# Stationary operands woven in pairs of blocks, and split weights placed at 128 modulo 256 bytes

## The chip, the cores and the metric

The kernel runs on one core of one Trainium2 chip. The metric is the device time of one execution in microseconds (us), as the median of several runs. Before the change it is 778.98 us (three runs, 777.98 to 779.29).

## The reference: what is computed

One encoder layer is applied to two sequences of 256 tokens with 1024 channels, all in fp32. The kernel treats them as one block of 512 tokens.

```
x = layer_norm(x)
z = x @ w_in + b_in                      # 1024 -> 3584, split into q, k, v, u_sg, v_sg, glu_a, glu_g
a = neighbourhood_attention(q, k, v) @ w_a_o
bb = (gelu(u_sg) * (w_s @ layer_norm(gelu(v_sg)) + b_s)) @ w_b_o
c = silu(layer_norm(conv31(glu_a * sigmoid(glu_g)))) @ w_c_o
g = sigmoid(x @ w_gate + b_gate)         # three gates of 1024
m = (g0 * a + g1 * bb + g2 * c) @ w_o + b_o
x = layer_norm(ALPHA * x + m)
f = top-2 of 16 experts (one group of 4): sum of gate_e * ((silu(x @ w_e1[e]) * (x @ w_e3[e])) @ w_e2[e])
y = layer_norm(ALPHA * x + f)
```

## The kernel before, in words

**One product is three.** The large products keep fp32 accuracy by splitting. A value x becomes `hi`, x rounded to the type fp32r, and `lo` = x - hi, also fp32r. A product is then hi·hi + hi·lo + lo·hi. The helper `three` issues these three matmuls in that order into one PSUM bank, 512 columns wide. Each matmul has its own load of the stationary operand, a block of 128 x 128 elements of 4 bytes, so 512 bytes in each partition. The moving operand has 128 x 512 elements, 2048 bytes in each partition.

**Weights come in units.** A unit is 1024 elements in each partition (512 KB in all). SyncE loads it into a raw buffer. ScalarE rounds it into a slot of `w_hi` (`cast_hi`, copy on L719), VectorE subtracts it into a slot of `w_lo` (`cast_lo`, L1055), and TensorE uses it. There are three slots of `w_hi` and `w_lo` for the mixer and a fourth (`w_hi_more`, `w_lo_more`) for the experts. Semaphores order the four: a raw buffer is loaded again after `lo_cast`, a slot is rounded into again after `unit_used`, and TensorE waits for `lo_cast` of the unit. The raw buffers are 6 in the mixer and a ring of 24 in the experts.

**Two ways of using a unit.** In `features` (units of the glu, q, k, u_sg, the gates and the branch projections) the weight is the stationary operand and the activation (`xT_hi`, `xT_lo`, `branch_hi`, `branch_lo`) is the moving one. A unit then holds eight blocks of 128 x 128. In `tokens` (units of v, v_sg, w_o and all experts) the weight is the moving operand, two chunks of 512 columns, and the activation is stationary: `xT_hi`/`xT_lo` for v and v_sg, `mT_hi`/`mT_lo` for w_o, `xgT_hi`/`xgT_lo` (the gathered tokens of an expert, transposed) for the first two matrices of an expert, `hT_hi`/`hT_lo` for the third.

**Where the operands lie.** Every stationary block is 128 elements next to one another. All the operands of `three` ask for an address that is a multiple of 256 bytes (`LINE = 256`), apart from `mT_lo` and the third branch, and blocks and chunks are multiples of 512 bytes apart.

**The order of work.** TensorE first transposes the input, then runs the units of `w_in` 0 to 27 (glu, v, v_sg, q and k, u_sg) with the attention and the spatial gating woven in between. Then come the gates and branches (`merge`, units 28 to 63), w_o (units 64 to 71), the router, and the 16 experts. An expert is 12 units of 6 matmuls, with two transposes of activations in between: `turn_xg` (L2137, eight of 128 columns) and `turn_h` (L2152, four). Their results are split by ScalarE (`split_xg` L932, `split_hT` L943) and VectorE (L1541, L1551). All orders are written out by hand, and each engine works through its own list in order. The depthwise convolution (31 taps, L1125) is done by VectorE in pieces between its weight subtractions.

The lines that the prediction speaks of: L1842 to L1844 (`three`), L1055 and L719 (the splits of weights), L2097 (`keep_busy`, matmuls whose result is not used, before the experts), L1985 (a plain fp32 product with `ones` for the mean of the convolution's normalisation), L565 (SyncE's loads), L1837 (`turn`, here the transposed softmax), L1888 (`attend`), L745 (ScalarE's sigmoid of the glu).

Of the kernel before, what the change touches and what calls it, by code (L numbers as in the profile page):

```python
# [56 lines left out]
LINE = 256  # L57
UNIT = 1024
# [103 lines left out]
def encoder_layer(nc, A, out_prompt, out_sample):  # L162
# [20 lines left out]
    w_hi = sb(ctx, "w_hi", [SPLIT, UNIT], F32R, LINE)  # L183
    w_lo = sb(ctx, "w_lo", [SPLIT, UNIT], F32R, LINE)
# [51 lines left out]
    mT_hi = sb(late, "mT_hi", [DC, T], F32R, LINE)  # L236
    mT_lo = sb(late, "mT_lo", [DC, T], F32R)
# [64 lines left out]
    list_row = sb(moe, "list_row", [EXPERTS], I32)  # L302
    list_gate = sb(moe, "list_gate", [EXPERTS])
    list_none = sb(moe, "list_none", [2, 4])
    list_base = sb(moe, "list_base", [2, 4])
    w_hi_more = sb(moe, "w_hi_more", [M_SPLIT - SPLIT, UNIT], F32R, LINE)
    w_lo_more = sb(moe, "w_lo_more", [M_SPLIT - SPLIT, UNIT], F32R, LINE)
# [5 lines left out]
    xgT_hi = sb(moe, "xgT_hi", [2, DC, SLOTS], F32R, LINE)  # L313
    xgT_lo = sb(moe, "xgT_lo", [2, DC, SLOTS], F32R, LINE)
    h_silu = sb(moe, "h_silu", [FF])
    h = sb(moe, "h", [FF])
    hT_hi = sb(moe, "hT_hi", [4, SLOTS], F32R, LINE)
    hT_lo = sb(moe, "hT_lo", [4, SLOTS], F32R, LINE)
# [102 lines left out]
    last_hT_hi, last_hT_lo = xgT_hi[:, 0, 0:4, :], xgT_lo[:, 0, 0:4, :]  # L421
# [276 lines left out]
    def _(act):  # L698
# [11 lines left out]
        def cast_hi(j, per=0, i=None):  # L710
# [8 lines left out]
            act.copy(hi_slot(j), raw_slot(j)).then_inc(hi_cast, 1)  # L719
# [117 lines left out]
        def merged_hi_rows(r):  # L837

            for c in (2 * r, 2 * r + 1):
                act.wait_ge(merged_ready, c + 1)  # L840
                act.copy(mT_hi[:, c, :], merged[:, c, :]).then_inc(merged_hi, 1)
# [99 lines left out]
        def split_hT(n, hT_hi=hT_hi[:]):  # L941
            act.wait_ge(*m_filled(M_HT, n))
            act.copy(hT_hi.rearrange("p c n -> p (c n)"), psum[M_HT][:]).then_inc(hT_hi_done, 1)  # L943
# [101 lines left out]
    def _(dve):  # L1045
# [37 lines left out]
        dve.tensor_copy(hi_slot(0), raw_slot(0)).then_inc(first_hi, 1)  # L1083
        dve.wait_ge(first_hi, 1)
        dve.tensor_tensor(lo_slot(0), raw_slot(0), hi_slot(0).bitcast(F32), ALU.subtract).then_inc(lo_cast, 1)
# [212 lines left out]
        def merged_lo_rows(r):  # L1298

            for c in (2 * r, 2 * r + 1):  # L1300
                dve.wait_ge(merged_hi, c + 1)
                dve.tensor_tensor(mT_lo[:, c, :], merged[:, c, :], mT_hi[:, c, :].bitcast(F32),
# [234 lines left out]
        def split_xg(n, q):  # L1537
            for half in range(2):
                dve.wait_ge(xg_hi, n * 2 + (half + 1))
                part_of = (slice(None), q, slice(4 * half, 4 * half + 4))  # L1540
                dve.tensor_tensor(xgT_lo[part_of], psum[M_XT + half][:].rearrange("p (c n) -> p c n", c=4),  # L1541
                                  xgT_hi[part_of].bitcast(F32), ALU.subtract).then_inc(psum_free[M_XT + half], 1)
# [6 lines left out]
        def split_hT(n, hT_hi=hT_hi[:], hT_lo=hT_lo[:]):  # L1549
            dve.wait_ge(hT_hi_done, n + 1)  # L1550
            dve.tensor_tensor(hT_lo.rearrange("p c n -> p (c n)"), psum[M_HT][:],  # L1551
                              hT_hi.rearrange("p c n -> p (c n)").bitcast(F32),
# [274 lines left out]
    def _(pe):  # L1827
# [18 lines left out]
        def features(j, outs, x_hi, x_lo, per=0, i=None):  # L1846

            pe.wait_ge(lo_cast, nth(j + 1, per, i))
            hi, lo = unit_of(hi_slot(j), len(outs) * P), unit_of(lo_slot(j), len(outs) * P)
            chunks = UNIT // (len(outs) * P)  # L1850
            for d, name in enumerate(outs):
                open_bank(name, i)
                cols = slice(d * P, (d + 1) * P)
                for c in range(chunks):
                    o = three(bank(name)[:], hi[:, c, cols], lo[:, c, cols], x_hi[:, c, :], x_lo[:, c, :],
# [3 lines left out]
        def tokens(j, k, last, outs, x_hi, x_lo, choose, per=0, i=None):  # L1859
# [3 lines left out]
            for t, out in enumerate(outs):  # L1863
                for c in range(2):
                    o = three(out, choose(x_hi[:, 2 * k + c, :], t), choose(x_lo[:, 2 * k + c, :], t), hi[:, c, :],
# [26 lines left out]
        def in_row(x, t):  # L1892
            return x[:, tokens_of(t)]

# [419 lines left out]
```

## Time and profile before

| | |
|---|---|
| median of three runs | 778.98 us |
| the profiled execution: its time | 777.9 us |
| its span, first to last instruction | 776.1 us |
| PE busy | 745.4 us (96%), 3516 matmuls |
| PEld (weight loads) busy | 616.5 us (79%) |
| DVE busy | 609.9 us (79%) |
| ACT busy | 432.6 us (56%) |
| mean granted TensorE clock | 0.992 |

PE is TensorE's matmuls and PEld its weight loads, DVE is VectorE, ACT ScalarE, POOL GpSimd and SPq the queue of SyncE. A matmul's recorded duration overlaps the next one, so the pace of the stream is read from the distance between starts, not from the durations. Of the 3516 matmuls 2880 are from `three`.

### The profile page before, as it was taken

What the parts mean: (1) busy time and instruction counts of PE and PEld (TensorE: products, weight loads), DVE (VectorE), ACT (ScalarE), POOL (GpSimd) and SP (SyncE); (2) the same over time, 40 slices, a digit from 0 to 9 for tenths busy, and PEclk for the clock granted to TensorE, in tenths of its full rate; (3) what the DMA queues carried; (4) which work ended last, traced back from release to release, by engine and by line L of the source; (5) the groups of instructions that cost most, each with busy time, mean ns of one, the idle gap of its engine ahead of it and who ended that gap; (6) DMA issues with size and microseconds to landing.
All of it is one profiled execution on the core that took longest, in us unless ns stands there. A gap on an engine that the chain in (4) does not pass through costs nothing.

```text
span 776.1 us, 10638 instructions
## 1 busy us (share of the span) xinstructions
PE 745.4 (96%) x3516; PEld 616.5 (79%) x3516; DVE 609.9 (79%) x827; ACT 432.6 (56%) x585; POOL 72.0 (9%) x96
## 2 busy tenths in 40 slices
PE   4999999999999999999999979999999999999995
PEld 3888877887888888888888857888888888888873
DVE  5799977777678857444348888999999999999977
ACT  5522235657322335422421456888888888888851
POOL 5000000000000000000011121111111111110314
PEclk9999999999999999999999989999999999999998
DMA  9744657232343452332388587999999999999682
GB/s 297 238 98 108 204 147 205 71 93 84 109 134 109 112 167 74 115 103 88 104 303 300 186 302 255 351 392 379 388 386 389 391 400 384 381 394 378 146 171 111
DMA packets 137489, 175.51 MB, mean 226 GB/s; under 512 B 15419, under 2 KB 75559, under 8 KB 137431
## 3 DMA queue, kind: packets, MB, share of 16 engines
q1 hardware_dynamic: 128896, 154.95, 58.8%
q0 software_dynamic: 7616, 19.34, 8.3%
q10 hardware_dynamic: 934, 0.69, 0.3%
q8 instruction: 23, 0.38, 0.2%
q14 instruction: 20, 0.16, 0.1%
HBM read 164.06 MB, written 19.11 MB: 236 GB/s over the span
## 4 chain that ended last, share of the span: by engine, by line
PE 85%; DVE 8%; DMA 2%; ACT 2%; SPq 2%; issue 1%; POOL 0%; DVEq 0%; ACTq 0%; POOLq 0%
PE bank L1842 25%; PE bank L1844 25%; PE bank L1843 25%; DVE w_lo L1055 2%; PE bank L2137 2%; DMA raw<-in_w_in_dram 2%; SPq L606 1%; DVE conv L1125 1%; DVE conv_odd L1125 1%; PE bank L2058 1%; PE bank L1837 1%; PE bank L2152 1%; PE bank L2238 1%; PE bank L1888 1%; PE bank L1904 1%
## 5 line engine op out<-in xcount | busy, mean ns | idle before, releaser
L1055 DVE TENSOR_TENSOR w_lo<-raw,w_hi 128x1024 fp32r<-128x1024 f32 x103 | 125.0, 1220 | 77.2 <-ACT w_hi L719 77.1
L719 ACT CAST w_hi<-raw 128x1024 fp32r<-128x1024 f32 x103 | 107.0, 1048 | 101.5 <-PE bank L1844 97.6
L1842 PE MATMUL bank<-xT_hi,w_hi 128*128 128x512 f32 x352 | 138.5, 393 | 2.7 <-DVE xT_lo L1093 1.5
L1844 PE MATMUL bank<-xT_hi,w_lo 128*128 128x512 f32 x352 | 137.1, 390 | 0.0
L1843 PE MATMUL bank<-xT_lo,w_hi 128*128 128x512 f32 x352 | 137.0, 389 | 0.0
L1842 PE MATMUL bank<-w_hi,xgT_hi 128*128 128x512 f32 x198 | 80.1, 405 | 1.0 <-issue 1.0
L1842 PEld LDWEIGHTS bank<-xT_hi,w_hi 128*128 128x128 f32 x352 | 66.1, 188 | 17.3 <-issue 3.1
L1844 PE MATMUL bank<-w_hi,xgT_lo 128*128 128x512 f32 x198 | 77.5, 391 | 0.0
L1843 PE MATMUL bank<-w_lo,xgT_hi 128*128 128x512 f32 x198 | 77.3, 390 | 0.0
L1844 PEld LDWEIGHTS bank<-xT_hi,w_lo 128*128 128x128 f32 x352 | 66.1, 188 | 14.0
L1843 PEld LDWEIGHTS bank<-xT_lo,w_hi 128*128 128x128 f32 x352 | 66.1, 188 | 13.4
L834 ACT ACTIVATE gate<-bank,vec 128x512 f32<-128x512 f32 x24 | 16.5, 689 | 83.2 <-PE bank L1844 83.2
L1055 DVE TENSOR_TENSOR w_lo<-raw_more,w_hi 128x1024 fp32r<-128x1024 f32 x40 | 48.2, 1221 | 5.7 <-ACT w_hi L719 5.4
L1055 DVE TENSOR_TENSOR w_lo<-raw_late,w_hi 128x1024 fp32r<-128x1024 f32 x40 | 48.2, 1220 | 4.1 <-ACT w_hi L719 3.9
L1125 DVE SCALAR_TENSOR_TENSOR conv<-conv_in,conv_col,conv 128x512 f32<-128x512 f32 x60 | 44.6, 744 | 0.0
L719 ACT CAST w_hi<-raw_more 128x1024 fp32r<-128x1024 f32 x40 | 41.2, 1049 | 4.5 <-PE bank L1844 4.5
L1844 PEld LDWEIGHTS bank<-w_hi,xgT_lo 128*128 128x128 f32 x198 | 37.2, 188 | 7.9
L1842 PEld LDWEIGHTS bank<-w_hi,xgT_hi 128*128 128x128 f32 x198 | 37.3, 188 | 7.8 <-issue 1.2
L719 ACT CAST w_hi<-raw_late 128x1024 fp32r<-128x1024 f32 x40 | 41.2, 1050 | 2.5 <-PE bank L1844 2.5
L1843 PEld LDWEIGHTS bank<-w_lo,xgT_hi 128*128 128x128 f32 x198 | 37.3, 188 | 6.6
L1125 DVE SCALAR_TENSOR_TENSOR conv_odd<-conv_in,conv_col,conv_odd 128x512 f32<-128x512 f32 x56 | 41.6, 744 | 0.0
L1055 DVE TENSOR_TENSOR w_lo<-raw_rows,w_hi 128x1024 fp32r<-128x1024 f32 x32 | 38.3, 1218 | 0.0
(289 smaller groups left out, 1530.9 us busy)
## 6 DMA issues: line engine op xcount, KB each, us to landing
raw_more<-in_w_e_dram SPq DMA_DIRECT2D x48, 512.0 KB, 7.0
raw<-in_w_e_dram SPq DMA_DIRECT2D x48, 512.0 KB, 7.9
raw_late<-in_w_e_dram SPq DMA_DIRECT2D x48, 512.0 KB, 7.1
raw_rows<-in_w_e_dram SPq DMA_DIRECT2D x48, 512.0 KB, 7.9
raw<-in_w_in_dram SPq DMA_DIRECT2D x28, 512.0 KB, 6.5
raw<-in_w_gate_dram SPq DMA_DIRECT2D x24, 512.0 KB, 3.7
y_scratch<-zeros SPq DMA_DIRECT2D x8, 512.0 KB, 5.3
raw<-in_w_o_dram SPq DMA_DIRECT2D x8, 512.0 KB, 3.8
```

The costliest lines, as they stand in the source:

```text
L606: sp.dma_start(v_win[:, seq, j, :], v_grid[:, WINDOW[j]:WINDOW[j] + KCOLS, :]).then_inc(v_windows, 16)
L719: act.copy(hi_slot(j), raw_slot(j)).then_inc(hi_cast, 1)
L834: act.activation(gate[:, n if n < 2 else r % 2, d, :], bank(name)[:], ACT.Sigmoid, bias=column(V_GATE + n * DC + 2 * r + d)).then_inc(free ...
L1055: dve.tensor_tensor(lo_slot(j), raw_slot(j), hi_slot(j).bitcast(F32), ALU.subtract).then_inc(lo_cast, 1)
L1125: o = dve.scalar_tensor_tensor(out=sum_, in0=shifted, scalar=conv_col[:, k, c:c + 1], in1=sum_, op0=ALU.mult, op1=ALU.add)
L1837: o = pe.transpose(bank(name)[:, k * P:(k + 1) * P], tile(k), ident)
L1842: pe.matmul(out, hi_l, hi_r, start=start, stop=False)
L1843: pe.matmul(out, hi_l, lo_r, start=False, stop=False)
L1844: return pe.matmul(out, lo_l, hi_r, start=False, stop=stop)
L1888: o = pe.matmul(bank(("attended", g))[:, j * P:(j + 1) * P], v_win[:, seq, j, hp * P:(hp + 1) * P], probsT[:, j * P:(j + 1) * P], start=Tr ...
L1904: o = pe.transpose(bank(name)[:, tokens_of(t)], x_in[:, t, c * P:(c + 1) * P], ident)
L2137: o = pe.transpose(psum[M_XT + half][:, k * P:(k + 1) * P], xg[:, q, c * P:(c + 1) * P], ident)
```

## The change

Two blocks of a stationary operand are stored element by element: element n of block 2k lies at 2n and element n of block 2k+1 at 2n+1. A load of one block then reads every second element, 128 elements over 1024 bytes. This holds for the weights of `features` (they are woven where they are split) and for `mT_hi`, `xgT_hi`, `xgT_lo`, `hT_hi` and `hT_lo`. The stationary operands `xT_hi`, `xT_lo` (for v and v_sg) and `mT_lo` stay as they were, and so do the weights where they are moving operands. `w_hi`, `w_lo`, `w_hi_more` and `w_lo_more` now ask for a multiple of 128 bytes; with the order in which they are placed they lie at 128 modulo 256. All other operands of `three` stay at multiples of 256.

```diff
+APART = 128
-    w_hi = sb(ctx, "w_hi", [SPLIT, UNIT], F32R, LINE)
-    w_lo = sb(ctx, "w_lo", [SPLIT, UNIT], F32R, LINE)
+    w_hi = sb(ctx, "w_hi", [SPLIT, UNIT], F32R, APART)
+    w_lo = sb(ctx, "w_lo", [SPLIT, UNIT], F32R, APART)
-    mT_hi = sb(late, "mT_hi", [DC, T], F32R, LINE)
-    mT_lo = sb(late, "mT_lo", [DC, T], F32R)
+    mT_hi = sb(late, "mT_hi", [DC // 2, T, 2], F32R, LINE)
+    mT_lo = sb(late, "mT_lo", [DC, T], F32R, LINE)
...
-    xgT_hi = sb(moe, "xgT_hi", [2, DC, SLOTS], F32R, LINE)
+    xgT_hi = sb(moe, "xgT_hi", [2, DC // 2, SLOTS, 2], F32R, LINE)
-    hT_hi = sb(moe, "hT_hi", [4, SLOTS], F32R, LINE)
+    hT_hi = sb(moe, "hT_hi", [2, SLOTS, 2], F32R, LINE)
...
+    def is_stationary(j):
+        return j < U_V or U_QK <= j < U_WO
+    def woven(slot):
+        return slot.rearrange("p (k n b) -> p k b n", b=2, n=P)
+    def split_of(slot, j):
+        return woven(slot) if is_stationary(j) else slot
+    def raw_of(j):
+        return raw_slot(j).rearrange("p (k b n) -> p k b n", b=2, n=P) if is_stationary(j) else raw_slot(j)
+    def chunk(tile, c):
+        return tile[:, c // 2, :, c % 2]
+    def by_chunk(tile):
+        return tile.rearrange("p k n b -> p k b n")
...
-            act.copy(hi_slot(j), raw_slot(j)).then_inc(hi_cast, 1)
+            act.copy(split_of(hi_slot(j), j), raw_of(j)).then_inc(hi_cast, 1)
...
-            dve.tensor_tensor(lo_slot(j), raw_slot(j), hi_slot(j).bitcast(F32),
+            dve.tensor_tensor(split_of(lo_slot(j), j), raw_of(j), split_of(hi_slot(j).bitcast(F32), j),
...
-                act.copy(xgT_hi[:, q, 4 * half:4 * half + 4, :],
-                         psum[M_XT + half][:].rearrange("p (c n) -> p c n", c=4)).then_inc(xg_hi, 1)
+                act.copy(by_chunk(xgT_hi[:, q, 2 * half:2 * half + 2]),
+                         psum[M_XT + half][:].rearrange("p (k b n) -> p k b n", k=2, b=2)).then_inc(xg_hi, 1)
...
-            hi, lo = unit_of(hi_slot(j), len(outs) * P), unit_of(lo_slot(j), len(outs) * P)
+            hi, lo = woven(hi_slot(j)), woven(lo_slot(j))
...
-                    o = three(bank(name)[:], hi[:, c, cols], lo[:, c, cols], x_hi[:, c, :], x_lo[:, c, :],
+                    at = (slice(None), *divmod(len(outs) * c + d, 2))
+                    o = three(bank(name)[:], hi[at], lo[at], x_hi[:, c, :], x_lo[:, c, :],
                               c == 0, c == chunks - 1)
...
-            tokens(j, k, k == 3, [psum[b][:]], xgT_hi[:, q], xgT_lo[:, q], lambda x, t: x, per, i)
+            tokens(j, k, k == 3, [psum[b][:]], chunks_of(xgT_hi[:, q]), chunks_of(xgT_lo[:, q]), whole, per, i)
```

The splits of `mT`, `xgT_lo` and `hT` are changed in the same way. No instruction is added, taken away or moved, and no semaphore changes.

## Rows read from the trace of the kernel before

**Rows 1.** The page, busy time and share of the span by engine.
```profile
PE 745.4 (96%) x3516; PEld 616.5 (79%) x3516; DVE 609.9 (79%) x827; ACT 432.6 (56%) x585; POOL 72.0 (9%) x96
```

**Rows 2.** Waits of PE: engine, line, releaser: us in total, times, longest.
```profile
PE bank L1888 <- DVE branch_lo L1169: 1.8, 1, 1.8
...
PE bank L1837 <- DVE probs L1162: 1.0, 1, 1.0
```

**Rows 3.** Groups of PE by line: busy, mean ns, idle before and its releasers.
```profile
L1842 PE MATMUL bank<-xT_hi,w_hi 128*128 128x512 f32 x352 | 138.5, 393 | 2.7 <-DVE xT_lo L1093 1.5 <-DVE vs L1217 1.0 <-DVE w_lo L1055 0.2
```

**Rows 4.** Timeline of PE (start us, us), 24 matmuls in a row, first and last.
```profile
225.21 0.39 PE L1842 MATMUL bank<-branch_hi,w_hi 128*128 128x512 f32 x1
...
230.43 0.39 PE L1844 MATMUL bank<-branch_hi,w_lo 128*128 128x512 f32 x1
```

**Rows 5.** Timeline of PE, one unit of `features` behind a transpose.
```profile
140.83 0.40 PE L1843 MATMUL bank<-xT_lo,w_hi 128*128 128x512 f32 x1
...
141.53 0.39 PE L1843 MATMUL bank<-xT_lo,w_hi 128*128 128x512 f32 x1
141.75 0.39 PE L1844 MATMUL bank<-xT_hi,w_lo 128*128 128x512 f32 x1
...
142.91 0.39 PE L1843 MATMUL bank<-xT_lo,w_hi 128*128 128x512 f32 x1
...
144.95 0.39 PE L1843 MATMUL bank<-xT_lo,w_hi 128*128 128x512 f32 x1
```

**Rows 6.** Timeline of PE, a plain fp32 product's two records.
```profile
274.17 0.59 PE L1985 MATMUL bank<-conv_ln,const 128*128 128x512 f32 x1
...
274.60 0.59 PE L1985 MATMUL bank<-conv_ln,const 128*128 128x512 f32 x1
```

**Rows 7.** Timeline of PE, two looks at L2097, five starts apart.
```profile
462.78 1.05 PE L2097 MATMUL bank<-w_hi 128*128 128x512 f32 x2
...
464.91 1.05 PE L2097 MATMUL bank<-w_hi 128*128 128x512 f32 x2
```

**Rows 8.** Windows, L2097 alone: PE busy (x), PEld busy (x), PEclk, DMA share, GB/s.
```profile
463.30:465.90 2.60, 2.60 (x8) 2.02 (x7) 0.50 0.54 148
```

**Rows 9.** Timeline of PE, eight transposes of 128 columns.
```profile
466.41 1.03 PE L2137 MATMUL bank<-const,xg 128*128 128x128 f32 x8
```

**Rows 10.** Windows by stage, L1842 alone, columns as in rows 8.
```profile
20.00:63.00 43.00, 24.48 (x63) 11.82 (x63) 1.00 0.58 160
63.00:131.00 68.00, 37.39 (x96) 17.83 (x95) 1.00 0.62 173
131.00:172.00 41.00, 16.09 (x40) 7.52 (x40) 1.00 0.31 91
...
190.00:431.00 241.00, 136.39 (x348) 65.34 (x348) 1.00 0.46 144
431.00:468.00 37.00, 4.88 (x12) 2.25 (x12) 0.91 0.68 244
468.00:752.00 284.00, 152.19 (x384) 72.18 (x384) 1.00 0.98 351
```

**Rows 11.** Chain that ended last, 18 to 110 us and 110 to 200 us.
```profile
63.12 0.70 ACT tmp L745
...
105.34 13.78 DMA raw<-in_w_in_dram
...
172.28 1.34 ACT probs L771 x7
```

**Rows 12.** Windows, all engines (PE, PEld, DVE, ACT, POOL busy), a stretch of experts.
```profile
550.00:600.00 50.00, 50.00 (x236) 41.60 (x235) 46.81 (x49) 43.12 (x52) 5.04 (x5) 1.00 1.03 389
```

**Rows 13.** Waits of SyncE's queue.
```profile
SPq L565 <- DVE w_lo L1055: 378.9, 178, 9.3
```

**Rows 14.** Groups by line, columns as in rows 3.
```profile
L2137 PE MATMUL bank<-const,xg 128*128 128x128 f32 x128 | 16.5, 272 | 0.0
...
L1055 DVE TENSOR_TENSOR w_lo<-raw,w_hi 128x1024 fp32r<-128x1024 f32 x103 | 125.0, 1220 | 77.2 <-ACT w_hi L719 77.1
```

More of the change, by code:

```diff
@@ L418, in encoder_layer @@
     out_stored = sem("out_stored")
[L421 removed]
+    last_hT_hi, last_hT_lo = xgT_hi[:, 0, 0:2], xgT_lo[:, 0, 0:2]
     turned = [next_turned[:, 0], onehot[:, 1]]
@@ L1539, in split_xg @@
                 dve.wait_ge(xg_hi, n * 2 + (half + 1))
-                part_of = (slice(None), q, slice(4 * half, 4 * half + 4))
-                dve.tensor_tensor(xgT_lo[part_of], psum[M_XT + half][:].rearrange("p (c n) -> p c n", c=4),
-                                  xgT_hi[part_of].bitcast(F32), ALU.subtract).then_inc(psum_free[M_XT + half], 1)
+                part_of = (slice(None), q, slice(2 * half, 2 * half + 2))
+                dve.tensor_tensor(by_chunk(xgT_lo[part_of]),
+                                  psum[M_XT + half][:].rearrange("p (k b n) -> p k b n", k=2, b=2),
+                                  by_chunk(xgT_hi[part_of].bitcast(F32)),
+                                  ALU.subtract).then_inc(psum_free[M_XT + half], 1)
         def gate_h(unit, n):
@@ L1864, in tokens @@
                 for c in range(2):
-                    o = three(out, choose(x_hi[:, 2 * k + c, :], t), choose(x_lo[:, 2 * k + c, :], t), hi[:, c, :],
+                    o = three(out, choose(x_hi(2 * k + c), t), choose(x_lo(2 * k + c), t), hi[:, c, :],
                               lo[:, c, :], k == 0 and c == 0, last and c == 1)
@@ L1893, in in_row, with whole, chunks_of, rows_of @@
             return x[:, tokens_of(t)]
+        def whole(x, t):
+            return x
+        def chunks_of(tile):
+            return lambda c: chunk(tile, c)
+        def rows_of(tile):
+            return lambda c: tile[:, c, :]
         pe.wait_ge(const_loaded, 16)
@@ L1925, in first_units @@
                 open_bank(name)
-            hi, lo = unit_of(hi_slot(u), P), unit_of(lo_slot(u), P)
+            hi, lo = woven(hi_slot(u)), woven(lo_slot(u))
             for c in chunks:
                 pe.wait_ge(*drained(("x0T", c)))
-                o = three(bank(name)[:], hi[:, c, :], lo[:, c, :], xT_hi[:, c, :], xT_lo[:, c, :], c == 0,
+                o = three(bank(name)[:], hi[:, c // 2, c % 2], lo[:, c // 2, c % 2], xT_hi[:, c, :], xT_lo[:, c, :], c == 0,
                           c == DC - 1)
@@ L1948, in _ @@
                         open_bank(("v", t))
-                tokens(u, u - U_V, u == U_V + 3, [bank(("v", t))[:] for t in range(TT)], xT_hi, xT_lo, in_row)
+                tokens(u, u - U_V, u == U_V + 3, [bank(("v", t))[:] for t in range(TT)],
+                       rows_of(xT_hi), rows_of(xT_lo), in_row)
             elif u < U_QK:
@@ L1953, in _ @@
                         open_bank(("vsg", t))
-                tokens(u, u - U_VSG, u == U_VSG + 3, [bank(("vsg", t))[:] for t in range(TT)], xT_hi, xT_lo, in_row)
+                tokens(u, u - U_VSG, u == U_VSG + 3, [bank(("vsg", t))[:] for t in range(TT)],
+                       rows_of(xT_hi), rows_of(xT_lo), in_row)
             elif u < U_USG:
@@ L2016, in _ @@
                 pe.wait_ge(merged_lo, 2 * k + 2)
-                tokens(U_WO + 4 * n + k, k, k == 3, [bank(("mixed", n, t))[:] for t in range(TT)], mT_hi, mT_lo,
-                       in_row)
+                tokens(U_WO + 4 * n + k, k, k == 3, [bank(("mixed", n, t))[:] for t in range(TT)],
+                       chunks_of(mT_hi), rows_of(mT_lo), in_row)
         def mix_out(t):
@@ L2027, in mix_out @@
                 for c in range(2):
-                    o = three(bank(name)[:], in_row(mT_hi[:, 2 * k + c, :], t), in_row(mT_lo[:, 2 * k + c, :], t),
+                    o = three(bank(name)[:], in_row(chunk(mT_hi, 2 * k + c), t), in_row(mT_lo[:, 2 * k + c, :], t),
                               hi[:, c, :], lo[:, c, :], False, k == 3 and c == 1)
@@ L2160, in output @@
                 pe.wait_ge(*m_empty(M_Y + k // 2, n))
-            tokens(j, k % 2, k % 2 == 1, [psum[M_Y + k // 2][:]], hT_hi, hT_lo, lambda x, t: x, per, i)
+            tokens(j, k % 2, k % 2 == 1, [psum[M_Y + k // 2][:]], chunks_of(hT_hi), chunks_of(hT_lo), whole, per, i)
         pe.wait_ge(routed, 1)
```

24 lines of the change are left out of this document (12 added, 12 removed).

## The prediction

> **What bounds the kernel now.** I read the busy times first: TensorE is busy for 745.4 of 776.1 us [rows 1]. Then its waits: two in the middle are 1.8 and 1.0 us [rows 2], and its largest group waited for a split of weights for 0.2 us in all [rows 3]. So nothing feeds TensorE too late, and the pace of its own stream sets the time. The pace stands in the timeline, as the distance between starts. Over 24 matmuls of `three` it is (230.43 - 225.21) / 23 = 226.9 ns [rows 4]. 512 columns at the full clock of 2.4 GHz are 213.3 ns, so each pair of load and matmul takes about 13.5 ns more than its columns. 2880 pairs times that are 39 us. This is all that the change can reach, since no instruction goes.
>
> **What the excess is.** Three readings bear on it.
> First, it is absent at half clock. L2097 has the same pairs with its weights contiguous, the granted clock there is 0.50 [rows 8], and five starts take 464.91 - 462.78 = 2.13 us, 426 ns each [rows 7], which is 512 columns at 1.2 GHz and nothing more. A fixed price for changing the weights would show there too.
> Second, it isn't constant. Behind a transpose nine starts take 142.91 - 140.83 = 2.08 us, 231 ns each, with one of 220 (141.53 to 141.75), and the next nine 144.95 - 142.91 = 2.04 us, 227 ns each [rows 5]. Same shapes, same operands: what differs is when the load runs relative to the matmul.
> Third, where no new weights are needed between two passes of 512 columns, it is nearly gone. A plain fp32 product's two records are 430 ns apart [rows 6], which I take as two passes on the same weights: 215 ns each.
> All three fit two reads of the on-chip memory that get into each other's way while a weight load runs beside a matmul. Eight transposes of 128 columns take 1.03 us [rows 9]; without the last one's duration of 0.272 [rows 14] the seven steps are 108 ns each, where 128 columns would take 53. So a load takes about 107 ns and walks its 512 bytes at 4.8 bytes per ns, while the moving operand is walked at 4 bytes x 2.4 GHz = 9.6. Two walks at unequal speed, both from multiples of 256 bytes, must pass through each other.
>
> The Trainium skill says otherwise: by "TensorE: Matmul & The Clock Gate", section "Step-by-step: what each phase is for", the streaming operand and the weight load have independent read ports, and the load of the next weights takes no read bandwidth from the running matmul. By that the excess would be something else and the change would leave it at 226.9 ns and the time at 779. The rows on phase and clock [rows 5, 7] speak against it; it stands below as the case of no change.
>
> **The change part by part.**
> 1. The weave. A load of 128 elements now covers 1024 bytes in the same 107 ns: 9.6 bytes per ns, the moving operand's own speed. With the split weights at 128 modulo 256 and the other operand at 0, the two reads stay 128 bytes apart modulo 256 all the way, if they start together. Woven are all stationary blocks but those of v and v_sg (192 pairs) and `mT_lo` (64). If memory is split by that bit of the address, they never meet, and the pair falls to the 215 ns of [rows 6]: 226.7 - 215 = 11.7 ns gained (226.7 for the steady steps, between 226.9 and 226.7 of [rows 4] and [rows 5]). Bounds: 13.4 ns gained (bare columns); below, a loss of 11.7, if the price goes by the memory that a load touches, which doubles. I take 11.7, as the row of passes without a load is the nearest to a load that meets nothing.
> 2. Where the gain arrives. L1842 is a third of the pairs, so its loads by stage [rows 10] times three: 20 to 63 us: 189; 131 to 172: 120; 190 to 431: 1044, less the 64 of `mT_lo` 980; 431 to 468: 36; 468 to 752: 1152. Sum 2477, times 11.7 ns = 29.0 us.
> 3. Where it doesn't. From 63.12 the chain runs through ScalarE, then VectorE's convolution and SyncE's and the DMA's work until 119.1 (105.34 + 13.78) [rows 11], and ends in the softmax's wait of 1.0 us [rows 2]. None of that gets faster, so the 285 pairs in 63 to 131 (95 of them woven) only make that wait longer. The same holds from 172.28 [rows 11], where ScalarE and VectorE carry the chain to the wait of 1.8 us [rows 2]: 48 pairs, 0.6 us. I count both at nothing; cover that is gone can't hurt, as TensorE is the one that comes early.
> 4. The splits. `cast_hi`, `cast_lo` and the splits of `mT`, `xgT` and `hT` write every second element. A weight subtraction takes 1220 ns [rows 14] for 1024 contiguous elements; the trace has no written stride of this kind. Bounds: nothing, or twice the time. In the mixer a unit of 24 matmuls lasts 24 x 215 = 5.2 us, and TensorE waited 0.2 us for splits [rows 3], so 1.2 us more is mostly hidden, at most some us in the convolution's stage. Among the experts the weights are not woven; only six splits of 512 elements are. I take nothing.
> 5. What is late next. Among the experts VectorE is busy for 46.81 of 50 us [rows 12]. The stage of 284 us gets shorter by 1152 x 11.7 ns = 13.5 us, 4.7%, so VectorE's share rises from 94% to about 98%: it still fits, barely. SyncE waits 378.9 us in all for a free raw buffer [rows 13], so the loads run ahead by a full ring, and 389 GB/s needn't rise at once for weights to be there in time. I add nothing, and keep 2 us of the range for it.
>
> **The sum.** 777.9 (the profiled execution) - 29.0 = 748.9 us. The median of the runs lies 1.1 us above that execution, so 750.0 us.
>
> **The rivals.**
> - *Doubling.* The price goes by the lines of memory that a load touches, each of which holds up the matmul. A contiguous load touches 512 bytes for 11.7 ns, a woven one 1024 for 23.4. It decides if the two walks collide although they are 128 bytes apart. Pair: 238.4 ns. The 2477 pairs cost 29.0 us more, the 95 and 48 of part 3 1.7: 777.9 + 30.7 + 1.1 = 809.7 us, slower. For it: the excess is near to one cycle of 2.4 GHz for each 16 bytes of a load (32 x 0.417 = 13.3). Against it: such a price would be the same at every phase, and [rows 5] has 220 and more than 231 side by side.
> - *Half.* The walks start out of step, and part of each load still collides: half the gain, 14.5 us, 764.5 us.
> - *Nothing.* The excess belongs to the change of weights in the array at full clock, whatever the addresses: 779.0 us. For it: it is so steady at 226.7 for hundreds of pairs. Against it: the half clock.
> - *Slower splits.* Writes of every second element hold VectorE up between the end of v_sg and 131 us, where the chain goes through its splits: six woven units x 1.2 us = up to 7.2 us, and without a gain in the pairs that gives 786 us. It needs both, a split twice as long and no gain.
>
> Of the doubling the Trainium skill says, in "SBUF — State Buffer", section "Specifications (TRN2)", that lines are of 16 bytes and at least two hits in each give full bandwidth. Every second fp32 element is two hits in a line: by that rule a woven load is still at full speed, but at its edge. The trace of before has no strided load to show it.
>
> **How the numbers follow.** The forecast has a chance of 0.52, half 0.10, nothing 0.15, doubling 0.17, slower splits 0.06. So faster 0.62, same 0.15, slower 0.23; 0.2% (1.6 us) is about what a measurement of this kernel can tell from no change. The forecast's own range is 743 (13.4 ns on 2477 pairs is 33.2 us, with the unsteady steps gone another 2) to 755 (the experts' VectorE at 2 us, a rest of 1.5 ns in each pair). The range of 8 in 10 reaches from 743 over half and nothing to 784; the doubling and the worst of the splits lie outside.
>
> **What would show it.** Right: starts of L1842 to L1844 about 215 ns apart at 225 us and among the experts, but still near 227 in v and v_sg (63 to 106 us) or less if the shift by 128 alone helps; longer waits of PE at L1837 and L1888; VectorE's share near 98% among the experts. Doubling would show as 238 ns at full clock; nothing as 226.7 with the same waits; slower splits as longer L1055 and L719 and a wait of L1842 for `w_lo`. The forecast is wrong if the distance of starts does not fall where blocks are woven.

## The result, and the profile after

| | before | after |
|---|---|---|
| median | 778.95 us | 792.0 us |
| lowest to highest of four runs | 777.98 to 779.29 | 791.63 to 792.44 |
| span of the profiled execution | 776.1 us | 789.8 us |
| ratio, 95% interval | | 1.017, 1.0152 to 1.0187 |

The change makes the kernel 13.1 us slower, where 29 us of gain were forecast (750.0 us, with a range of 743 to 784).

The profile's page has the busy times of the changed kernel, which answer to [rows 1]. As many matmuls and loads as before; TensorE is busy for 13.6 us more, VectorE and ScalarE for a little more.

```profile
PE 759.0 (96%) x3516; PEld 638.5 (81%) x3516; DVE 611.5 (77%) x827; ACT 438.0 (55%) x585; POOL 72.0 (9%) x96
```

The waits of TensorE, which answer to [rows 2], are no longer than they were; of its others two at the start grew, from 9.5 to 9.7 us for `x_in` and from 1.5 to 1.8 us for `xT_lo`. So the time did not go into a new wait.

```profile
PE bank L1916 <- DVE branch_lo L1195: 1.8, 1, 1.8
...
PE bank L1865 <- DVE probs L1188: 0.7, 1, 0.7
```

The pace is where it went. The timeline of TensorE (start, duration, both in us) shows, by their first and last matmuls, a stretch of v, whose stationary operand is not woven; the stretch of `features` of [rows 4]; and a stretch among the experts. Before and behind the latter stand two landmarks, the experts' first transposes and the first product behind the experts. In these lines the moving operand is named first and the stationary one second.

```profile
80.09 0.40 PE L1870 MATMUL bank<-w_hi,xT_hi 128*128 128x512 f32 x1
...
83.83 0.40 PE L1871 MATMUL bank<-w_lo,xT_hi 128*128 128x512 f32 x1
...
225.39 0.39 PE L1870 MATMUL bank<-xT_hi,w_hi 128*128 128x512 f32 x1
...
230.70 0.39 PE L1872 MATMUL bank<-branch_hi,w_lo 128*128 128x512 f32 x1
...
475.03 1.38 PE L2176 MATMUL bank<-const,xg 128*128 128x128 f32 x8
...
501.77 0.39 PE L1872 MATMUL bank<-w_hi_more,hT_lo 128*128 128x512 f32 x1
...
504.55 0.39 PE L1872 MATMUL bank<-w_hi,xgT_lo 128*128 128x512 f32 x1
...
766.48 1.02 PE L2277 MATMUL bank<-x,const 128*128 128x512 f32 x2
```

In v, 16 steps take 3.74 us, 233.8 ns each. In `features`, 23 steps take 230.70 - 225.39 = 5.31 us, 230.9 ns each, where [rows 4] has 226.9. Among the experts, 12 steps take 2.78 us, 231.7 ns each. The durations (0.39) hardly tell of it; the starts do.

The two landmarks place the loss. The transposes stood at 466.41 in [rows 9], so 8.6 us are lost ahead of the experts. The first product behind them (here L2277, before L2238) is at 752.67 in the timeline of before, so 13.8 us are lost by then, 5.2 of them among the experts: 1152 pairs at 4.5 ns each.

About one of the 8.6 us comes of the clock and not of where the operands lie. The windows of TensorE show the same stretch before and after (length, busy time and count, granted clock, DMA share, GB/s):

```profile
18.36:21.77 3.41, 3.19 (x13) 1.00 1.07 299
...
18.36:21.77 3.41, 3.41 (x9) 0.50 1.01 290
```

In the profiled execution of the changed kernel nine steps run there at some 427 ns, the pace of a granted clock of 0.50. The transposes of `w_s`, which follow, come at 29.73 us before and at 30.94 after, but at 29.87 in the first experiment below, which weaves too and has a granted clock of 1.00 in this stretch. The second experiment has such a stretch, the others don't. No run shows whether the change brings it about.

The other engines. The splits keep pace: the weight subtraction takes 1222 ns, where [rows 14] has 1220, and from 250 to 400 us, where nearly all of it is woven, 1224 against 1222. ScalarE's rounding of weights (L744) takes 1112 ns in the same stretch, where the unwoven one took 1043. VectorE waits for it a little longer (82.7 us in all, 77.1 in [rows 14]), but TensorE waits for neither. Among the experts VectorE is busy for 45.81 of 50 us (46.81 in [rows 12]), since its work is spread over more time, and SyncE's wait for raw buffers is 390.8 us (378.9 in [rows 13]).

```profile
L1080 DVE TENSOR_TENSOR w_lo<-raw,w_hi 128x1024 fp32r<-128x1024 f32 x103 | 125.2, 1222 | 83.5 <-ACT w_hi L744 82.7
```

```profile
L744 ACT CAST w_hi<-raw 128x1024 fp32r<-128x1024 f32 x27 | 30.0, 1112 | 25.7 <-PE bank L1872 25.7
```

```profile
550.00:600.00 50.00, 50.00 (x234) 42.58 (x233) 45.81 (x48) 42.60 (x51) 6.05 (x6) 1.00 1.02 372
```

```profile
SPq L590 <- DVE w_lo L1080: 390.8, 178, 9.4
```

### The profile page after: what moved, and what is told of

Same layout as the page of the kernel before. It is cut to its first block, busy times and chain, and to the rows that moved or that the text cites. A ratio compares the mean times of both kernels' runs of the same rounds, so it can differ in the third digit from the quotient of the medians.

```text
span 789.8 us, 10638 instructions
## 1 busy us (share of the span) xinstructions
PE 759.0 (96%) x3516; PEld 638.5 (81%) x3516; DVE 611.5 (77%) x827; ACT 438.0 (55%) x585; POOL 72.0 (9%) x96
## 4 chain that ended last, share of the span: by engine, by line
PE 92%; DVE 4%; ACT 2%; issue 1%; DMA 1%; POOL 0%; ACTq 0%; DVEq 0%; POOLq 0%
PE bank L1870 27%; PE bank L1871 27%; PE bank L1872 27%; PE bank L2176 2%; PE bank L2097 1%; PE bank L1865 1%; PE bank L2191 1%; PE bank L2277 1%; PE bank L1916 1%; PE bank L1941 1%; DVE w_lo L1080 1%; DMA x_in<-in_x_prompt_dram 1%; PE bank L2136 1%; PE bank L1906 1%; ACT w_hi L744 1%
## 5 line engine op out<-in xcount | busy, mean ns | idle before, releaser
L1080 DVE TENSOR_TENSOR w_lo<-raw,w_hi 128x1024 fp32r<-128x1024 f32 x103 | 125.2, 1222 | 83.5 <-ACT w_hi L744 82.7
L744 ACT CAST w_hi<-raw 128x1024 fp32r<-128x1024 f32 x103 | 111.2, 1089 | 102.9 <-PE bank L1872 100.6
L1870 PE MATMUL bank<-xT_hi,w_hi 128*128 128x512 f32 x352 | 140.4, 399 | 2.8 <-DVE xT_lo L1119 1.8
L1871 PE MATMUL bank<-xT_lo,w_hi 128*128 128x512 f32 x352 | 139.3, 396 | 0.0
L1872 PE MATMUL bank<-xT_hi,w_lo 128*128 128x512 f32 x352 | 139.1, 395 | 0.0
L1870 PEld LDWEIGHTS bank<-xT_hi,w_hi 128*128 128x128 f32 x352 | 69.3, 197 | 15.7 <-issue 3.4
L1872 PEld LDWEIGHTS bank<-xT_hi,w_lo 128*128 128x128 f32 x352 | 69.4, 197 | 12.7
L1871 PEld LDWEIGHTS bank<-xT_lo,w_hi 128*128 128x128 f32 x352 | 69.3, 197 | 12.1
L1080 DVE TENSOR_TENSOR w_lo<-raw_late,w_hi 128x1024 fp32r<-128x1024 f32 x40 | 48.2, 1222 | 5.2 <-ACT w_hi L744 4.4
L1872 PEld LDWEIGHTS bank<-w_hi,xgT_lo 128*128 128x128 f32 x198 | 38.9, 196 | 7.1
L744 ACT CAST w_hi<-raw_more 128x1024 fp32r<-128x1024 f32 x40 | 41.0, 1045 | 4.7 <-PE bank L1872 4.7
L744 ACT CAST w_hi<-raw_late 128x1024 fp32r<-128x1024 f32 x40 | 41.1, 1047 | 2.7 <-PE bank L1872 2.7
```

The costliest lines, as they stand in the source:

```text
L744: act.copy(split_of(hi_slot(j), j), raw_of(j)).then_inc(hi_cast, 1)
L1080: dve.tensor_tensor(split_of(lo_slot(j), j), raw_of(j), split_of(hi_slot(j).bitcast(F32), j), ALU.subtract).then_inc(lo_cast, 1)
L1870: pe.matmul(out, hi_l, hi_r, start=start, stop=False)
L1871: pe.matmul(out, hi_l, lo_r, start=False, stop=False)
L1872: return pe.matmul(out, lo_l, hi_r, start=False, stop=stop)
```

## The experiments

Three explanations were open. **By place:** each pair has a price that is set by how its two operands lie, the distance of their addresses modulo 256 bytes and the stride of the load; the kernel of before sits on a cheap arrangement. (A place is an address modulo 256 bytes; "64 against 0" is a stationary operand at 64 and a moving one at 0.) **By footprint:** a woven load costs more because it touches twice the memory, wherever it lies; then the shift is free. **By waits:** the splits with a stride hold something up.

### The weave without the shift

From the changed kernel, with all weights back at 0 modulo 256:

```diff
-APART = 128
+APART = 256
```

(`w_hi_more` and `w_lo_more` also go back behind `list_base`.)

> The weave is kept, all split weights lie at 0 modulo 256 bytes as before the change. Theory A (the shift of the weights against the other operand costs, the weave is neutral): the steps of three stay at 226.7 ns where blocks are woven, time 778 to 781 us. Theory B (the weave costs, because a load touches twice the memory): steps of 230 ns or more where blocks are woven and 226.7 in v and v_sg, time 788 to 794 us. If the two streams collide more when they are in step and at the same address modulo 256, the steps are above 231 ns and the time is above 792.

Measured: 795.11 us (795.02 to 795.63) beside 778.68 for the kernel before; ratio 1.0212, interval 1.0195 to 1.0229. The timeline has a stretch of v, 24 steps, and the stretch of `features`, 12 steps:

```profile
80.02 0.39 PE L1872 MATMUL bank<-w_hi,xT_lo 128*128 128x512 f32 x1
...
85.46 0.39 PE L1872 MATMUL bank<-w_hi,xT_lo 128*128 128x512 f32 x1
...
225.27 0.39 PE L1871 MATMUL bank<-xT_lo,w_hi 128*128 128x512 f32 x1
...
228.07 0.39 PE L1871 MATMUL bank<-xT_lo,w_hi 128*128 128x512 f32 x1
```

2.80 / 12 = 233.3 ns where the load is woven; 5.44 / 24 = 226.7 ns in v, where neither stride nor place has changed. The weave alone costs 16.4 us, more than the whole change. So the shift does not add to it, it takes something off.

### The shift without the weave

From the kernel before, the split weights at 128 modulo 256 and nothing woven:

```diff
+APART = 128
-    w_hi = sb(ctx, "w_hi", [SPLIT, UNIT], F32R, LINE)
-    w_lo = sb(ctx, "w_lo", [SPLIT, UNIT], F32R, LINE)
+    w_hi = sb(ctx, "w_hi", [SPLIT, UNIT], F32R, APART)
+    w_lo = sb(ctx, "w_lo", [SPLIT, UNIT], F32R, APART)
```

(`w_hi_more` and `w_lo_more` likewise, in the changed kernel's order.)

> The split weights lie at 128 modulo 256 bytes, nothing is woven. Theory A (the shift costs): steps of 231 to 233 ns everywhere, as v and v_sg show them in the changed kernel (they are not woven and average 233), time 792 to 797 us. Theory B (the weave costs): steps of 226.7, time 778 to 781 us.

Measured: 793.96 us (792.63 to 794.33) beside 778.68; ratio 1.019, interval 1.0173 to 1.0207. Timeline, `features`, 24 steps:

```profile
225.32 0.39 PE L1844 MATMUL bank<-xT_lo,w_hi 128*128 128x512 f32 x1
...
230.89 0.40 PE L1844 MATMUL bank<-branch_lo,w_hi 128*128 128x512 f32 x1
```

5.57 / 24 = 232.1 ns with contiguous loads. The same instructions, the same bytes and no strided write anywhere: only the addresses moved, and 15.3 us are lost. That is against the footprint as the only cause, and waits can't explain it: TensorE's two are 1.6 and 0.6 us here, and the splits take 1223 and 1045 ns from 250 to 400 us, as before (1222 and 1043). The costs are not additive either: 16.4 and 15.3 us alone, 13.1 us together.

### The pairs by themselves

The next kernel does not compute the layer. It holds streams of 60 pairs of load and matmul with nothing else running on the core, each stream in one form:

```
l, r = blocks(stat_64, 1, 128), chunks(mov_0, 1, 512)   # stationary at 64, contiguous; moving at 0
for k in range(60):
    pe.matmul(psum[g][:], l[k % 4], r[k % 2], start=k == 0, stop=k == 59)
```

> A kernel of its own: 23 streams of 60 pairs of weight load and matmul with no other engine at work; each stream has its own stride of the stationary block and its own places of the two operands modulo 256 bytes. It does not compute the layer. If the excess over 213 ns is a collision of TensorE's own two reads, the contiguous stream at 0 against 0 shows 226.7 ns here too, and the step changes with stride and place; bf16, which reads half the bytes, shows 216 or less; loads of 64 and 32 columns show less excess in proportion. If it comes from the other engines' use of the memory, all streams here show 213 to 216. Theory A: contiguous 128 against 0 is 231 or more, every second 0 against 0 is 226.7. Theory B: every second is 230 or more at all places, every fourth more still.

In the timeline each stream is one row, and the step is the distance to the next row's start divided by 60. The rows are: contiguous with the stationary operand at 64 (L81), 128 (L84) and 192 (L87) against a moving one at 0; woven at 0 (L90), 32 (L93), 128 (L99) and 192 (L102); both operands at 128 (L117); the same block each time (L120); bf16 contiguous (L129) and woven (L132); fp32r with a moving operand of every second element (L135); and 256 moving columns (L138).

```profile
42.15 14.16 PE L81 MATMUL bank<-mov,stat 128*128 128x512 f32 x60
56.15 14.11 PE L84 MATMUL bank<-mov,stat 128*128 128x512 f32 x60
70.10 13.90 PE L87 MATMUL bank<-mov,stat 128*128 128x512 f32 x60
83.83 14.16 PE L90 MATMUL bank<-mov,stat 128*128 128x512 f32 x60
97.83 14.07 PE L93 MATMUL bank<-mov,stat 128*128 128x512 f32 x60
...
125.55 14.05 PE L99 MATMUL bank<-mov,stat 128*128 128x512 f32 x60
139.44 14.16 PE L102 MATMUL bank<-mov,stat 128*128 128x512 f32 x60
...
209.79 13.79 PE L117 MATMUL bank<-mov,stat 128*128 128x512 f32 x60
223.43 13.77 PE L120 MATMUL bank<-mov,stat 128*128 128x512 f32 x60
...
264.73 13.12 PE L129 MATMUL bank<-movb,statb 128*128 128x512 bf16 x60
277.69 13.11 PE L132 MATMUL bank<-movb,statb 128*128 128x512 bf16 x60
290.45 27.41 PE L135 MATMUL bank<-mov,stat 128*128 128x512 f32 x60
317.69 7.38 PE L138 MATMUL bank<-mov,stat 128*128 128x256 f32 x60
```

Contiguous: 14.00 / 60 = 233.3 ns at 64, 232.5 at 128, 228.8 at 192. Woven: 233.3 at 0 and 13.89 / 60 = 231.5 at 128, the changed kernel's own pace. Both operands at 128: 13.64 / 60 = 227.3, and 226.7 once settled (the last 40 steps), as with both at 0; so it is the difference of the two places that counts. Loads of 64 and 32 columns, for which less excess was expected in proportion, settle at 229.9 and 231.7 ns. bf16 takes 216.0 ns (12.96 / 60), and the weave changes nothing there: 215.8 settled for both. With 256 moving columns and both at 0 the settled step is 120.0 ns, and 256 columns are 106.7, so the excess is 13.3 ns, the same as for 512 at these places.

The view of one line gives the loads' own durations (minimum, median, maximum in ns): contiguous (L78), every second element (L90), every fourth (L105).

```profile
L78 PEld LDWEIGHTS bank<-mov,stat x60: 187/188/188, 27.9 to 41.7; 128*128 128x128 f32 x60
...
L90 PEld LDWEIGHTS bank<-mov,stat x60: 193/193/194, 83.6 to 97.4; 128*128 128x128 f32 x60
...
L105 PEld LDWEIGHTS bank<-mov,stat x60: 308/309/311, 153.2 to 167.1; 128*128 128x128 f32 x60
```

A woven load is hardly longer (193 against 188 ns). The Trainium skill, "SBUF — State Buffer", section "Specifications (TRN2)", asks for at least two hits in each line of 16 bytes; by that rule every second fp32 element is still at full speed and every fourth is not, and the loads agree (193, then 309 ns). But the pair pays more all the same, 233.3 against 226.7 ns. The same row of the Trainium skill says that each cross to a new line pays a penalty; it gives no size. A woven load crosses twice as often, but contiguous loads reach 233.4 ns by place alone, and bf16 pays nothing for the weave. So the lines alone don't set the price.

What follows: the price is there with nothing else on the core, so neither waits nor other engines make it, and place and stride both count.

### All places

The second kernel of streams, also without the layer, fills in the places.

> A kernel of its own as m1_streams, 23 streams of 60 pairs; it does not compute the layer. Theory C (the fp32 moving operand is read at the very limit of TensorE's read path, so that a stall at a change of weights is never made up; its size depends on the places of the two operands modulo 256 bytes): bf16 with every second element moving asks for the same bytes per ns as fp32 and shows an excess of 10 ns or more over 213 (bf16 contiguous showed 215.8), bf16 with every fourth takes about twice 213 ns; 384 moving columns take 173.3 ns (160 + 13.3), 256 columns with a load of 32 take 120 to 125; contiguous at 256 against 0 gives 226.7 again. Theory D (the excess belongs to the type fp32r and its weight loads, not to the bytes of the moving operand): bf16 with every second element moving stays at 215.8. Neither says which place is best; places other than a difference of 0 are expected between 227 and 236 ns, and one below 226.7 would point to a kernel faster than before.

With the last of them from the next such kernel, the settled steps in ns are these, for a stationary operand at that place modulo 256 against a moving one at 0:

```
place        0     16    32    48    64    80    96    112
contiguous   226.7 233.3 233.4 233.3 233.4 231.9 234.3 233.3
every second 233.3 233.3 232.0 231.1 230.1 232.1 233.3 230.1

place        128   144   160   176   192   208   224   240
contiguous   232.4 233.4 233.3 229.8 228.9 233.3 233.3 226.7
every second 231.5 233.4 233.3 233.3 233.3 231.6 233.3 231.4
```

The means are close, 231.9 contiguous and 232.3 woven. What sets them apart is that the contiguous load has places that cost nothing more, 0 and 240, and the kernel of before stands on one; the woven load has none (230.1 at best). Nothing in the table is below 226.7. The cheap places are narrow: contiguous loads at 8, 232 and 248, also measured, take 230.7, 231.1 and 233.3 ns. One expectation failed: loads of 32 columns against 256 moving ones take 117.8 ns, not 120 to 125. And 128, the place furthest from the moving operand, is one of the dear ones.

### The place 192, in the whole kernel

The table says that 192 is a cheap shift for `features` (228.9; only 240 is cheaper) and, as a difference of 64, a dear one where the activation is stationary (233.4). From the kernel before:

```diff
+    pad = sb(ctx, "pad", [16], F32, 128)
-    w_hi = sb(ctx, "w_hi", [SPLIT, UNIT], F32R, LINE)
-    w_lo = sb(ctx, "w_lo", [SPLIT, UNIT], F32R, LINE)
+    w_hi = sb(ctx, "w_hi", [SPLIT, UNIT], F32R, 64)
+    w_lo = sb(ctx, "w_lo", [SPLIT, UNIT], F32R, 64)
```

(`w_hi_more` and `w_lo_more` also at 192, behind `list_gate`.)

> Nothing is woven, all split weights lie at 192 modulo 256 bytes, the other operands at 0. Theory C' (the step of a pair is set by the difference, stationary place less moving place, modulo 256 bytes, as in the streams): where the weight is stationary the difference is 192 and the step 229 ns (it was 228.9 in the stream), where the weight is moving the difference is 64 and the step 233.4. Sum: 1344 pairs x 2.2 ns + 1536 x 6.7 ns = 13.2 us, less what two stages hide (about 2): 778.7 + 11 = 790 us. A rival (only whether the places are equal counts, any difference costs the same): all steps about 232.5 and 794 us.

Measured: 789.74 us (789.0 to 790.71) beside 778.95; ratio 1.0143, interval 1.0125 to 1.0161. Timeline, v and `features`, 24 steps each:

```profile
79.82 0.39 PE L1843 MATMUL bank<-w_hi,xT_hi 128*128 128x512 f32 x1
...
85.42 0.39 PE L1843 MATMUL bank<-w_hi,xT_hi 128*128 128x512 f32 x1
...
225.31 0.39 PE L1845 MATMUL bank<-xT_hi,w_lo 128*128 128x512 f32 x1
...
230.80 0.39 PE L1845 MATMUL bank<-branch_hi,w_lo 128*128 128x512 f32 x1
```

5.49 / 24 = 228.8 ns in `features` and 5.60 / 24 = 233.3 ns in v. The same two buffers are cheap in one role and dear in the other, as the table has it, and the time is the 790 us expected from it. The rival, by which any difference of places costs the same, gave 794.

### Only the activations woven

From the kernel with the weave and no shift, so that the weights of `features` lie as before:

```diff
     def woven(slot):
-        return slot.rearrange("p (k n b) -> p k b n", b=2, n=P)
+        return slot.rearrange("p (k b n) -> p k b n", b=2, n=P)
```

> All split weights lie at 0 modulo 256 bytes and are stored as before the change; only the activations that are stationary (mT_hi, xgT, hT) are woven. If the price of the weave is paid pair by pair: 226.7 ns in the units where the weight is stationary, 233.3 where a woven activation is (1152 pairs of the experts and 128 of w_o), 1280 x 6.6 = 8.4 us, 787 us, half of what the whole weave costs at the same places (16.4 us). If the price came from the woven writes of weights or from their reads by another engine, this kernel would be at 779.

Measured: 787.5 us (786.74 to 788.05) beside 778.95; ratio 1.0108, interval 1.009 to 1.0126. Timeline, `features` (24 steps) and experts (15 steps):

```profile
225.31 0.39 PE L1870 MATMUL bank<-branch_hi,w_hi 128*128 128x512 f32 x1
...
230.75 0.39 PE L1870 MATMUL bank<-xT_hi,w_hi 128*128 128x512 f32 x1
...
499.82 0.39 PE L1872 MATMUL bank<-w_hi,xgT_lo 128*128 128x512 f32 x1
...
503.32 0.39 PE L1872 MATMUL bank<-w_hi,xgT_lo 128*128 128x512 f32 x1
```

5.44 / 24 = 226.7 ns where nothing is woven, 3.50 / 15 = 233.3 where it is. The price sits where woven blocks are used and not where the weights are written or read by others. (The pairs of `mT_lo`, contiguous but between woven ones, pay as well: 233.7 ns in the table below.)

All whole kernels can now be put side by side. The mean step in ns of the pairs of `three` by kind, from the records of each trace (steps of 260 ns and more left out, which are waits, transposes and other products in between, or steps at half clock), and the sum over kinds of count x (step - step of before), where the count is that of the steps of before that are left, against the measured difference of medians:

```
kernel               features  v,v_sg  tokens  mT_lo |  sum   measured
(count)              1325      191     1243    63    |  us    us
before               227.1     226.7   227.4   227.7 |
after                231.4     233.3   231.7   232.2 |  12.5  13.1
weave, no shift      233.5     226.7   234.2   233.6 |  17.2  16.4
shift 128, no weave  232.8     233.3   232.7   233.1 |  15.6  15.3
shift 192, no weave  229.0     233.3   233.4   233.1 |  11.6  10.8
activations woven    227.1     226.7   234.2   233.7 |   8.7   8.6
```

"tokens" are the pairs with `mT_hi`, `xgT` or `hT` stationary. The sums come within 0.8 us of the measured times; taken over all 2880 pairs they are 0.3 to 0.5 us higher and come within 1.2. To that precision the pairs' steps are the whole effect.

### What the excess belongs to

> A kernel of its own, streams of 60 pairs (15 for plain fp32); it does not compute the layer. Only the difference of the places counts: 64 against 64 shows 226.7, 64 against 192 and 0 against 128 alike (232.4 to 233.4), 192 against 128 as 64 against 0 (233.4), 0 against 64 as 192 against 0 (228.9). Plain fp32, whose records lie 429 ns apart in the kernel: if its moving operand is read at half the rate (4.8 bytes per ns), places change nothing, the weave changes nothing, and a moving operand of every second element costs nothing either; if it is read at the full rate and merely meets no load, every second element doubles it to 850. bf16 with every second element moving was 225.8 at 16-byte loads per 8 elements; woven stationary there stays within 2 ns of it, and a load of 32 columns too, if the excess comes from the start of each matmul and not from the length of the load. No place of a woven load is below 230, none of a contiguous one below 226.7.

This kernel of streams also leaves the layer out. Its rows: both operands at 64, then 64 against 192; and, further on, 192 against 128, plain fp32 contiguous, plain fp32 with the load at 128, plain fp32 woven, plain fp32 with a moving operand of every second element, and the start of bf16 with both operands of every second element.

```profile
162.25 13.78 PE L131 MATMUL bank<-mov,stat 128*128 128x512 f32 x60
175.88 14.16 PE L134 MATMUL bank<-mov,stat 128*128 128x512 f32 x60
...
203.62 14.16 PE L140 MATMUL bank<-mov,stat 128*128 128x512 f32 x60
217.61 13.04 PE L143 MATMUL bank<-movf,statf 128*128 128x512 f32 x30
230.49 13.04 PE L146 MATMUL bank<-movf,statf 128*128 128x512 f32 x30
243.36 13.04 PE L149 MATMUL bank<-movf,statf 128*128 128x512 f32 x30
256.24 13.66 PE L152 MATMUL bank<-movf,statf 128*128 128x512 f32 x30
269.74 13.66 PE L155 MATMUL bank<-movb,statb 128*128 128x512 bf16 x60
```

Both at 64: 13.63 / 60 = 227.2 with its first steps, 226.7 settled. 64 against 192 settles at 233.4, 0 against 64 at 228.9, 192 against 128 at 233.3. The last two are what 192 against 0 and 64 against 0 gave: the difference modulo 256 decides. One pair stands out by 1 ns: 0 against 128 has 233.4, 128 against 0 has 232.4.

Plain fp32 (each matmul is two records, with a load each) takes 12.88 / 30 = 429.3 ns a record wherever its load lies, and woven too. That is [rows 6]'s 430, and it does not answer to what an fp32r pair answers to. With a moving operand of every second element a record takes 13.50 / 30 = 450 ns, 21 more, while the same step takes an fp32r matmul from 227 to 451 ns (27.24 / 60 = 454 with the first steps). So, if a record is two passes as the prediction took it, a pass of the plain product does not read its moving operand as an fp32r pass does.

The bf16 streams say the same from the other side. Settled steps: contiguous 215.8 ns; with a moving operand of every second element, which covers as many bytes per column as fp32r does, 225.8; with the load moved to 128, 225.0; with the load woven too, 225.0; with loads of 32 columns, 225.0. Here the load has next to no say, and some 10 ns of excess are there as soon as the moving operand covers 2048 bytes.

> A kernel of its own, 23 streams of 60 pairs; it does not compute the layer. Question: where does the excess over 213 ns arise, and what does the place act on? If the load's reads collide with the matmul's one by one over the load's length, loads of 32 columns are all alike at the four places (within 1 ns of the 231.7 at 0) and the spread over the places grows with 64 and 96 columns. If the place acts at the change from one matmul to the next, loads of 32 and 64 columns spread over the places as loads of 128 do (227 to 233 ns). Matmuls of 256 columns: excess of 13 to 20 ns over 106.7 as with 512, with 128 against 0 worse than 0 against 0 (120.0). Every fourth: no place below 233, and with 256 moving columns its load, which had a duration of 309 ns against 188, becomes the bound and the step rises above 200 ns.

The last kernel, streams without the layer, varies the length of the load. Loads of 32 columns at 0, and the start of the next stream:

```profile
25.27 14.06 PE L70 MATMUL bank<-mov,stat 128*32 128x512 f32 x60
39.16 14.06 PE L73 MATMUL bank<-mov,stat 128*32 128x512 f32 x60
```

13.89 / 60 = 231.5 ns, above the 226.7 of a load four times as long. Over the places 0, 64, 128 and 192 the settled steps are:

```
load of      at 0   at 64  at 128  at 192  spread
32 columns   231.6  231.6  230.6   231.6    1.0
64 columns   230.3  232.7  229.4   228.4    4.3
96 columns   230.0  228.3  231.5   233.3    5.0
128 columns  226.7  233.4  232.4   228.9    6.7
```

The spread grows with the load, as it should if two reads meet while a load lasts. But which place is cheap changes with the length (0 for 128 columns, 64 for 96, 192 for 64), and the shortest load still takes 17 to 18 ns over its columns at all four places. Two woven loads of 64 columns are cheaper than contiguous ones at the same place: 226.7 against 232.7 ns at 64, 228.8 against 229.4 at 128. For the kernel's own form, 128 columns against 512, no place or stride that was tried is below 226.7, and before stands there.

With 256 moving columns the places rank the other way round, against the expectation. Loads of 128 columns at 64 (L112), and the start of those at 128:

```profile
218.78 7.24 PE L112 MATMUL bank<-mov,stat 128*128 128x256 f32 x60
225.85 7.28 PE L115 MATMUL bank<-mov,stat 128*128 128x256 f32 x60
```

7.07 / 60 = 117.8 ns. Settled, the places 64, 128 and 192 take 117.8, 118.6 and 117.8 ns, less than the 120.0 of both at 0. So the excess over the columns is not one fixed sum either: 11.1 ns at 64. With loads of 32 columns at 0 it is 6.7 ns for 128 moving columns (60.0 - 53.3), 11.1 for 256 (117.8 - 106.7) and 18.3 for 512 (231.6 - 213.3).

## Why the prediction was wrong

**What the excess is.** This step failed, in its third reading. The 215 ns of [rows 6] were taken for two passes over one set of weights, and hence for the price of a pair whose load meets nothing. The streams of plain fp32 show a pass that is indifferent to the load's place and stride, and reads its moving operand in another way than an fp32r pass. It is no bound for a pair. The first two readings hold as observations: no excess at half clock (the first steps of the stream kernels are 426.7 ns too, at 0, 8 and 16 against 0 alike), and a step that isn't constant [rows 5]. But that the whole 13.5 ns is collision does not follow from them. The forecast needed the step to fall to 215 ns; the fp32r streams with 512 contiguous moving columns lie between 226.7 and 240.0 at every place, stride and load length tried. "A fixed price for changing the weights would show there too", at half clock, was argued and not measured. What no place took away is there at full clock alone, so its absence at half clock does not mark it as a collision.

**Part 1, the weave.** Two things were wrong. The gain of 11.7 ns a pair wasn't there to be had. And "if memory is split by that bit of the address, they never meet" is not borne out: at 128 against 0 the woven pair costs 231.5 ns and the contiguous one 232.4. For contiguous loads the step had the direction of the shift reversed, since equal places give the 226.7. For woven ones the shift does help, but by 1.8 ns (233.3 to 231.5; in the whole kernel 795.1 to 792.0 us), while the weave costs 6.6. I argued that two walks of unequal speed from multiples of 256 must pass through each other; the measured best is just that arrangement. What was missing was a price for it from a row, since every operand of before lay at 0 modulo 256 and the trace held no second place to compare.

**Part 2, where the gain arrives.** The count of pairs held, the sign and size per pair did not: -11.7 ns was forecast, +4.7 measured. 2477 pairs at +4.7 ns (231.4 - 226.7) would have given 11.6 us.

**v and v_sg.** "Near 227, or less if the shift alone helps" was given for the pairs without the weave. They went to 233.3: the shift moves their moving operand, and a contiguous load against a moving operand 128 bytes off costs 6.6 ns. I had counted the shift as harmless wherever it met no weave. These 192 pairs are 1.3 us.

**Parts 3 to 5.** Part 4 was right: strided writes cost VectorE 2 ns and ScalarE 69 ns of some 1050, behind other work. Parts 3 and 5 were not put to the test, as they say what happens to a gain. TensorE's two waits hardly moved (1.8 and 0.7 us), and VectorE's 98% among the experts did not come, as the stage got longer.

**The rivals.** Doubling had the sign and the part of the path, with a chance of 0.17, but its rule is refuted: it gave 238.4 ns and 809.7 us, and it would have the weave alone cost as much as the change and the shift nothing. The step of a woven pair depends on place (230.1 to 233.4 ns), and the shift has a price of its own. Slower splits is refuted by the durations. Nothing and half are refuted by the time.

The Trainium skill, "TensorE: Matmul & The Clock Gate", section "Step-by-step: what each phase is for", says that the next weights load over a port of their own and take nothing from the running matmul. For bf16 contiguous the streams agree (215.8 ns, woven or not). For fp32r they don't: with nothing else on the core the same two instructions take 226.7 to 234.3 ns by address alone. The measurement decides. Which path the two reads share, if any, no run here shows.

**What stays open.** What the excess is that no place or stride took away. With loads of 128 columns and both operands at 0 it is 13.3 ns for 256, 384 and 512 moving columns, so no price per column; but other places bring it down to 11.1 for 256, and short loads change it. bf16 pairs are some 12 ns above their columns too, once their moving operand takes every second element (225.0 to 225.8 ns), and it is seen only at full clock. No run here says what it is. Nor is there a rule for the table of places; it was measured, not derived. For 512 moving columns no arrangement was found below the one of before, so there was no better version to run.

## What to carry to other kernels

When every operand of a trace lies at the same place, the trace can't price another place: a kernel of a few streams of 60 pairs, one form each, gives the steps in one run, and five whole kernels had them within 1 ns in all kinds but the pairs of `mT_lo`, which alternate with woven loads (233.6 ns in the weave without the shift, where the stream of their own form has 226.7). For fp32r blocks of 128 columns against 512 moving ones keep the stationary and the moving operand at the same place modulo 256 bytes and the stationary block contiguous; for other shapes measure, as the cheap place is another one. Take no "free" price from an operation with another data type, however alike its record looks.

## What the runs showed of the hardware that was not expected

- An fp32r matmul with a moving operand of every second element takes 451 ns, twice 226.7; bf16 takes 225.8 for every second element and 453.3 for every fourth. By the two hits per line of the Trainium skill ("SBUF — State Buffer", "Specifications (TRN2)") fp32 at every second element would keep its full speed; for the moving operand it does not.
- An address alone moves the step of an fp32r pair by up to 7.6 ns, 226.7 to 234.3. With 256 moving columns instead of 512 the equal places are the dearest of the four measured (120.0 against 117.8 to 118.6).
- A load of every fourth element takes 309 ns by its record. Under a matmul of 512 columns the pair takes 234.9 to 240.0 ns; with 256 columns it takes 233.3 and not 120: half the columns gain nothing, so there the load sets the pace.
- Shorter loads don't help: 32 columns instead of 128 make a pair with both operands at 0 slower, 231.6 against 226.7 ns.
